# Raw rows transposed at the two feed-forward norms of a two-block model, with the inverse roots applied behind the products

## The reference

```python
# block 1 (D_FF = 2816)
h = h + concatenate([y_a, y_b, y_c]) @ w_out
hn = rms_norm(h, ffn_norm)               # h * rsqrt(mean(h*h) + eps) * gain
h = h + (silu(hn @ w_gate) * (hn @ w_up)) @ w_down
h = rms_norm(h, final_norm)
# block 2 (D_FF_2 = 4096)
x = x + mix @ w_out_2
h2 = rmsnorm(x, norm_mlp)
x = x + square(relu(h2 @ w_up_2)) @ w_down_2
```

## Time and profile before

| | us |
|---|---|
| median of three runs | 999.0 (997.72 to 999.48) |
| the profiled execution, its own time | 1003.03 |
| its span, first to last instruction | 1001.2 |
| TensorE busy | 931.7 (93%) |
| VectorE busy | 610.0 (61%) |
| ScalarE busy | 465.6 (47%) |
| GpSimd busy | 153.6 (15%) |

### The profile page before, as it was taken

One profiled execution on the slowest core, in us unless ns is written; L12 is line 12 of the kernel. 1 busy time (PEld: TensorE's weight loads), 2 busy tenths in 40 slices (PEclk: granted clock), 3 DMA queues, 4 the chain that ended last, 5 costly groups with the idle time before them and its releaser, 6 DMA issues. The chain is left out here.

```text
span 1001.2 us, 17392 instructions
## 1 busy us (share of the span) xinstructions
PE 931.7 (93%) x6836; PEld 826.8 (83%) x6836; DVE 610.0 (61%) x1288; ACT 465.6 (47%) x906; POOL 153.6 (15%) x111
## 2 busy tenths in 40 slices
PE   4999897999999969989699999898999979999998
PEld 2997686999999959879688888897888779999996
DVE  4557656556445577459877977626756656544553
ACT  5454545535444455363334674353453445444441
POOL 2000000000000014001775314000000004222321
PEclk9999998999999989999799999999999989999999
DMA  8540332564566434363432201202546436555451
GB/s 307 166 138 1 114 118 85 169 209 164 175 193 209 156 105 139 135 252 113 162 127 86 64 13 43 86 3 85 176 160 193 146 124 207 193 190 168 169 189 42
DMA packets 38677, 139.60 MB, mean 139 GB/s; under 512 B 4330, under 2 KB 4586, under 8 KB 38596
## 3 DMA queue, kind: packets, MB, share of 16 engines
q1 hardware_dynamic: 37184, 134.17, 39.8%
q10 hardware_dynamic: 884, 2.49, 0.7%
q0 software_dynamic: 528, 1.84, 0.6%
HBM read 137.39 MB, written 1.08 MB: 138 GB/s over the span
## 5 line engine op out<-in xcount | busy, mean ns | idle before, releaser
L1642 DVE TENSOR_TENSOR parts<-raw,parts 128x1024 fp32r<-128x1024 f32 (+1 forms) x227 | 291.1, 1319 | 170.5 <-ACT parts L1166 169.2
L1166 ACT ACTIVATE parts<-raw 128x1024 fp32r<-128x1024 f32 (+1 forms) x227 | 229.8, 1048 | 114.9 <-PE psum L504 104.9
L502 PE MATMUL psum<-hT,parts 128*128 128x256 f32 (+1 forms) x928 | 265.5, 286 | 10.2 <-DVE scr L2052 9.4
L503 PE MATMUL psum<-hT,parts 128*128 128x256 f32 (+1 forms) x928 | 264.1, 285 | 0.0
L504 PE MATMUL psum<-hT,parts 128*128 128x256 f32 (+1 forms) x928 | 262.3, 283 | 0.0
L502 PEld LDWEIGHTS psum<-hT,parts 128*128 128x128 f32 x928 | 176.6, 190 | 13.3 <-DVE scr L2052 9.6
L504 PEld LDWEIGHTS psum<-hT,parts 128*128 128x128 f32 x928 | 177.6, 191 | 0.0
L503 PEld LDWEIGHTS psum<-hT,parts 128*128 128x128 f32 x928 | 176.9, 191 | 0.5
L502 PE MATMUL psum<-parts,arena_r 128*128 128x512 f32 x344 | 137.1, 399 | 3.6 <-issue 3.0
L504 PE MATMUL psum<-parts,arena_r 128*128 128x512 f32 x344 | 136.5, 397 | 0.0
L503 PE MATMUL psum<-parts,arena_r 128*128 128x512 f32 x344 | 136.4, 396 | 0.0
(11 more groups left out here) (293 smaller groups left out, 1158.4 us busy)
## 6 DMA issues: line engine op xcount, KB each, us to landing
raw<-weights SPq DMA_DIRECT2D x247, 512.0 KB, 4.2
raw<-weights SPq DMA_DIRECT2D x4, 384.0 KB, 7.9
X<-x SPq DMA_DIRECT2D x2, 512.0 KB, 6.4
out<-X SPq DMA_DIRECT2D x2, 512.0 KB, 2.6
arena<-lines POOLq DMA_DIRECT2D x1, 768.0 KB, 10.3
cbuf<-consts ACTq DMA_DIRECT2D x1, 561.0 KB, 5.3
arena<-lines POOLq DMA_DIRECT2D x1, 544.0 KB, 7.6
arena<-params ACTq DMA_DIRECT2D x1, 512.0 KB, 9.0
```

Of the source, the lines that this page charges most:

```text
L502: mm(ps, a, c, start=start, stop=False)
L503: mm(ps, a, d, start=False, stop=False)
L1166: signal(A(split_slot(name)[0], whole_piece, ACT.Copy), "first_parts")
L1642: signal(V_.tensor_tensor(second, whole_piece, first.bitcast(F32), ALU.subtract), "split_vector")
```

## The change

The transposes at both feed-forward norms read X itself, before any scaling, and in two column halves. `first_rows(0)` (k = 0 to 3) is issued inside the second half of the projection, behind piece j = 2; `first_rows(1)` (k = 4 to 7) is issued inside the first product (`gate.0`), ahead of its k = 4. `last_rows` does the same in block 2, inside `out2_1` and `up2.0`. The residual adds and the copies out of PSUM follow in the same halves. The half sums and the inverse root come behind all copies.

In block 1 TensorE spreads the two columns of inverse roots over all partitions (`inverse_rows`: a column broadcast to 128 x 128 against the identity), behind `up1.0`. ScalarE copies this row tile of 256 columns twice side by side, and VectorE multiplies the whole bank `gu_f` (512 columns) by it into SBUF, ahead of silu. In block 2 the square of relu carries the factor twice, and the last residual multiplies by its square, one number per token.

```diff
-        ffn1 = lay(0, [("Xn", TT * D), ("sg", 4 * SEQ), ("v", 4 * SEQ)])
+        ffn1 = lay(0, [("Xn", TT * D), ("gu", 4 * 2 * SEQ), ("rows", 2 * SEQ)])
...
-            def feature_product(name, cols, ps, acts=hT):
+            def feature_product(name, cols, ps, acts=hT, ahead_of={}):
                 w = [half.rearrange("p (k n) -> p k n", k=KD) for half in split(name)]
                 for k in range(KD):
+                    if k in ahead_of:
+                        ahead_of[k]()
                     need(k)
...
+            def rows_turned(tag, job, nh):
+                for t in range(TT):
+                    freed(pe, job(nh, t))
+                transposes_of(X, lambda k: f"{tag}_{k}", ks=range(4 * nh, 4 * nh + 4))
+
+            def first_rows(nh):
+                rows_turned("norm2", lambda nh, t: f"o12_{nh}_{t}", nh)
+
+            out1_part(2, 0)
+            out1_part(2, 1, lambda: first_rows(0))
...
-            norm_turn("norm2", 1, ffn1["Xn"].rearrange("p (t n) -> p t n", t=TT))
...
+            def inverse_rows():
+                pe.wait_ge(sem("rms2"), 1)
+                ps = opened("rows2")
+                for t in range(TT):
+                    last = mm(ps[:, P * t:P * t + P], st[:, 4 + t:5 + t].to_broadcast([P, P]), ident, start=True, stop=True)
+                closed(last, "rows2")
...
-                done_with(f"gate.{f}", feature_product(f"gate.{f}", tok, ps[:, 0:SEQ]))
+                done_with(f"gate.{f}", feature_product(f"gate.{f}", tok, ps[:, 0:SEQ],
+                                                       ahead_of={4: lambda: first_rows(1)} if f == 0 else {}))
+                if f == 0:
+                    turn[0], turn[1] = 0, 4
                 closed(feature_product(f"up1.{f}", tok, ps[:, SEQ:2 * SEQ]), name)
                 piece_used[f"up1.{f}"] = name
+                if f == 0:
+                    inverse_rows()
...
+            def last_rows(nh):
+                rows_turned("norm4", lambda nh, t: f"o2_{nh}_{t}", nh)
+
+            two_tokens("out2_0", "o2_0", mixT)
+            two_tokens("out2_1", "o2_1", mixT, lambda: last_rows(0))
+            late_rows = {4: lambda: last_rows(1)}
...
# ScalarE, block 1
+            turned_out(lambda k: f"norm2_{k}", hT, SEQ, lambda k: par("ffn_norm")[:, k:k + 1])
             half_sums("sq2", lambda t, nh: f"o12_{nh}_{t}", ffn1["Xn"].rearrange("p (t n) -> p t n", t=TT))
-            second_tile("2", ffn1["Xn"].rearrange("p (t n) -> p t n", t=TT))
-            turned_out(lambda k: f"norm2_{k}", hT, SEQ, lambda k: par("ffn_norm")[:, k:k + 1])
...
+            full(act, "rows2")
+            rows = ffn1["rows"].rearrange("p (s n) -> p s n", s=2)
+            step_ = A(rows[:, 0, :], bank_of("rows2")[:, 0:SEQ], ACT.Copy)
+            signal(step_, "rows_out")
+            release(A(rows[:, 1, :], bank_of("rows2")[:, 0:SEQ], ACT.Copy), "rows2")
+            gu = ffn1["gu"].rearrange("p (s w n) -> p s w n", s=4, w=2)
             for f in range(FT1):
                 full(act, f"gu_{f}")
-                if f >= 4:
-                    freed(act, f"gu_{f - 4}")
-                signal(A(sg[:, f % 4, :], bank_of(f"gu_{f}")[:, 0:SEQ], ACT.Silu), "silu1")
                 freed(act, f"gu_{f}")
-                signal(A(aT[:, 0, f, :], v1[:, f % 4, :], ACT.Copy), "hidden1_first")
+                signal(A(gu[:, f % 4, 0, :], gu[:, f % 4, 0, :], ACT.Silu), "silu1")
+                act.wait_ge(sem("gated1"), f + 1)
+                signal(A(aT[:, 0, f, :], gu[:, f % 4, 1, :], ACT.Copy), "hidden1_first")
...
# VectorE, block 1
-            residual([(t, nh, f"o12_{nh}_{t}") for nh in range(2) for t in range(TT)])
-            norm_rows("norm2", ffn1["Xn"].rearrange("p (t n) -> p t n", t=TT), "sq2")
-            turned_rest(lambda k: f"norm2_{k}", hT, SEQ, lambda k: par("ffn_norm")[:, k:k + 1])
+            for nh in range(2):
+                residual([(t, nh, f"o12_{nh}_{t}") for t in range(TT)], nh == 0)
+                turned_rest(lambda k: f"norm2_{k}", hT, SEQ, lambda k: par("ffn_norm")[:, k:k + 1], range(4 * nh, 4 * nh + 4))
+            dve.wait_ge(sem("sq2"), 2 * TT)
+            link(V_.tensor_tensor(st[:, 0:2], st[:, 0:2], st[:, 2:4], ALU.add))
+            inv_rms(st[:, 4:6], st[:, 0:2], D, st[:, 6:8], st[:, 8:10], "rms2")
...
             def hidden_rest(f):
+                dve.wait_ge(sem("silu1"), f + 1)
+                u = gu[:, f % 4, 1, :]
+                signal(V_.tensor_tensor(u, u, gu[:, f % 4, 0, :], ALU.mult), "gated1")
                 dve.wait_ge(sem("hidden1_first"), f + 1)
-                signal(V_.tensor_tensor(aT[:, 1, f, :], v1[:, f % 4, :], aT[:, 0, f, :].bitcast(F32), ALU.subtract), "hidden1")
+                signal(V_.tensor_tensor(aT[:, 1, f, :], u, aT[:, 0, f, :].bitcast(F32), ALU.subtract), "hidden1")
+            freed(dve, "rows2")
             for f in range(FT1):
                 full(dve, f"gu_{f}")
-                dve.wait_ge(sem("silu1"), f + 1)
-                release(V_.tensor_tensor(v1[:, f % 4, :], bank_of(f"gu_{f}")[:, SEQ:2 * SEQ], sg[:, f % 4, :], ALU.mult),
-                        f"gu_{f}")
+                release(V_.tensor_tensor(ffn1["gu"].rearrange("p (s n) -> p s n", s=4)[:, f % 4, :], bank_of(f"gu_{f}"),
+                                         ffn1["rows"], ALU.mult), f"gu_{f}")
                 hidden_rest(f)
...
# VectorE, block 2: halves as above with o2_, norm4 and norm_mlp, then
+            inv_rms(st[:, 4:6], st[:, 0:2], D, st[:, 6:8], st[:, 8:10])
+            link(V_.tensor_tensor(st[:, 10:12], st[:, 4:6], st[:, 4:6], ALU.mult))
...
-            residual([(t, nh, f"d2_{t}_{nh}") for t in range(TT) for nh in range(2)])
+                    release(V_.scalar_tensor_tensor(out=xs, in0=bank_of(name), scalar=st[:, 10 + t:11 + t], in1=xs,
+                                                    op0=ALU.mult, op1=ALU.add), name)
```

More of the change, by code:

```diff
@@ L511, in need, with transposes_of @@
                     freed(pe, arrivals.pop(k))
-            def transposes_of(src, name_of, gain_tiles=KD, meta=None, turn_of=lambda k: ident):
-                for k in range(gain_tiles):
+            def transposes_of(src, name_of, meta=None, turn_of=lambda k: ident, ks=range(KD)):
+                for k in ks:
                     name = name_of(k)
@@ L534, in feature_product, with token_products @@
                 return last
-            def token_products(unit, tiles, acts, width=512):
+            def token_products(unit, tiles, acts, width=512, amid=None):
                 for job, cols in tiles:
@@ L553, in token_products @@
                         done_with(name, last)
+                    if j == 2 and amid:
+                        amid()
             def scores(g):
@@ L720, in y_turns, with out1_part @@
                     arrivals[k] = name
-            def out1_part(part, nh):
+            def out1_part(part, nh, amid=None):
                 js = OUT_PARTS[part]
@@ L741, in out1_part @@
                         done_with(name, last)
+                        if amid:
+                            amid()
             def swa_heads():
@@ L781, in _ @@
             y_turns(range(YM, KD))
-            for nh in range(2):
-                out1_part(2, nh)
+            def rows_turned(tag, job, nh):
[6 more added lines that the diff above has]
+            out1_part(2, 1, lambda: first_rows(0))
             def norm_turn(tag, count, src):
@@ L824, in down @@
                     done_with(f"{what}.{f}", last)
-            turn[0], turn[1] = 0, 4
+            def inverse_rows():
[4 more added lines that the diff above has]
+                closed(last, "rows2")
             def hidden1(f0, nf):
@@ L845, in _, with two_tokens @@
             norm_turn("norm3", 1, two["Xn"].rearrange("p (t n) -> p t n", t=TT))
-            def two_tokens(uname, tag, acts=hT):
-                token_products(uname, [(f"{tag}_{t}", tiles2[t]) for t in range(TT)], acts)
+            def two_tokens(uname, tag, acts=hT, amid=None):
+                token_products(uname, [(f"{tag}_{t}", tiles2[t]) for t in range(TT)], acts, amid=amid)
             def small_products():
@@ L1103, in _ @@
             transposes_of(mix, lambda k: f"mixT_{k}")
-            for n in range(2):
-                two_tokens(f"out2_{n}", f"o2_{n}", mixT)
-            norm_turn("norm4", 1, dn["Vb"].rearrange("p (t n) -> p t n", t=TT))
-            turn[0], turn[1] = 0, 4
+            def last_rows(nh):
[3 more added lines that the diff above has]
+            late_rows = {4: lambda: last_rows(1)}
             for n in range(8):
@@ L1112, in _ @@
                     ps = opened(name)
-                    done_with(f"up2.{2 * j}", feature_product(f"up2.{2 * j}", tok, ps[:, 0:SEQ]))
+                    done_with(f"up2.{2 * j}", feature_product(f"up2.{2 * j}", tok, ps[:, 0:SEQ],
+                                                              ahead_of=late_rows if j == 0 else {}))
+                    if j == 0:
+                        turn[0], turn[1] = 0, 4
```

(21 more changed lines are left out.)

5 lines of the change are left out of this document (1 added, 4 removed).

## The result

The changed kernel took 994.3 us (median of 10 runs, 989.8 to 996.2) beside 999.0 us before on the same chip (10 runs): ratio 0.9942, 95% interval 0.9923 to 0.9961. So it is faster, by 4.7 us; the forecast was 988.0 us and 11.0 us. In two further measurements beside the kernel before it took 991.3 and 995.6 us, ratios 0.9921 (0.9902 to 0.9940) and 0.9947 (0.9926 to 0.9967). Its 22 timed runs in these three measurements lie in two groups: ten at 989.8 to 992.5 us with a mean granted clock of 0.986 to 0.990, and twelve at 994.1 to 996.6 us with 0.979 to 0.983.

A forecast was written before the change was run, and what follows sets the result against it. TensorE, busy 93% of the span, was taken to bound the kernel, so only its gaps could be won. Terms -5.0 (first norm), -6.1 (second norm) and +0.1 (end) gave -11.0 from 999.0: 988.0 us, range 985.0 to 993.0.

The forecast's parts named there:

- First norm: Block 1's feed-forward norm: `gate.1` starts at 174.65 instead of 179.71, 5.0 us won.
- adds at 165.85: First norm: VectorE's two residual adds of columns 512 to 1023 start at 165.85, behind a weight split, and take 1.39 us.
- stall ahead of the roots: First norm, behind `up1.0`: TensorE waits 1.0 us for VectorE's inverse-root chain before the matmuls that spread the roots.
- the lower bound for the half sums: First norm, ScalarE: four half sums at 0.63 us each, ending at 171.8; 0 to 0.8 us more was possible.
- spreading matmuls: First norm: two matmuls spreading the inverse roots over the rows, taken as 0.25 us from two warm transposes.
- Second norm to `up2.1`: Block 2's feed-forward norm: the first product ends at 813.1 instead of 819.21, 6.1 us won.
- gate and up covered: Gate and up loop: VectorE needs at most 5.1 us of TensorE's 5.7 us per tile; the opposing rival had chance 0.04.
- the end: Last four residual adds, now with a per-partition factor: 0 to 0.07 us extra each, 0.1 us taken in all.
- clock rival at the norms: New short TensorE waits at the norms drop the clock, losing 2.2 us a norm: 990 to 992.5 us; chance 0.14.
- No spread of roots follows here: Second norm: sums and chain run beside products until about 817; only the last four adds want their factor.
- each microsecond saved at a norm moves the end by the same amount: Whole kernel: TensorE hardly waits elsewhere, so norm savings pass fully to the end if other engines keep up.
- the last line of the sum: Whole kernel: the summed change of -11.0 us taken from the timed 999.0 us, giving 988.0 us; chance 0.60.

The follow-up runs named there:

- bank kernel: Changed kernel with PSUM banks turned from 1, not 0, after the second norm's first up product: 988.92 us, then 992.73 us in a repeat.
- roots_later: Changed kernel with the two matmuls that spread the inverse roots one tile later, between `gate.1` and `up1.1`: 989.35 us.
- wide: Changed kernel with the 64-column matmuls behind norm 3 made 128 columns wide: 991.76 us, then 992.59 us in a repeat.
- first half: Changed kernel with its second norm and last adds put back as before the change: 995.85 us, ratio 0.9968.
- all four: Changed kernel with banks turned from 1, inverse roots one tile later, unread matmuls ahead of norm 3 and 128-column products behind it: 986.75 us.
- narrow later: Changed kernel with 8 unread 256-column matmuls ahead of the 64- and 128-column products behind norm 3, which so come 0.9 us later: 995.51 us.
- second half: Changed kernel with its first norm and gate and up loop put back as before the change: 995.24 us, ratio 0.9957.
- filler: Changed kernel with 60 unread 256-column matmuls in TensorE's wait ahead of norm 3's transposes: 990.31 us, ratio 0.9907.

## Why the prediction was wrong

**The local steps were right.** First norm: 5.0 us forecast, 5.1 measured. The single steps: adds at 165.85 forecast and 166.63 less 0.83 = 165.8 measured; 1.0 us of stall ahead of the roots forecast, 0.8 measured (174.96 less 174.04 less a pitch of 0.12; 0.64 of it put down to VectorE). The last half sum ended at 172.38 less 0.83 = 171.55, where 171.8 was reckoned, so the lower bound for the half sums was the right one. The spreading matmuls took 0.47 us (174.96 to 175.43), where 0.25 was reckoned from two transposes. These small errors cancel, by luck. Second norm to `up2.1`: 6.1 us forecast and measured. The 512-column product took 0.69 us, as taken from the add of the same shape; gate and up covered; the end 0.06 us a pair, 0.1 in all.

**The clock rival at the norms was wrong.** The short waits left the clock at the upper level in all profiles of the new form (twelve of each norm). The rule of the Trainium skill, "TensorE: Matmul & The Clock Gate", section "A second HAM failure mode: psum-queue depth-cycling", that frequent short idles make it swing, did not hold for these.

**One wait was missed.** "No spread of roots follows here" was true, but the bank counter is set back behind the first up product, and the first tile's bank is bank 0 already. Before, the reset stood ahead of it, and the two tiles had banks 0 and 1. The wait cost 0.84 us, and without it the bank kernel won 1.0.

**The step that failed** is the sentence "each microsecond saved at a norm moves the end by the same amount", and the last line of the sum, which took -11.0 from the median. The fixed part of the change is 207.24 - 202.19 = 5.05 us and 196.9 - 191.8 = 5.1 us, 10.15 in all. The time of the rest of the program isn't fixed:

```
profile            ahead of norm 1  low clock   middle  low clock   wait  middle less wait
roots_later             160.7          3.4       411.8    20.5      6.1       405.7
wide                    160.8          3.4       411.4    17.1      6.7       404.7
changed, third          161.5          6.8       416.9    27.3      8.3       408.6
before                  161.7          6.8       413.9    20.5      9.4       404.5
changed, second         161.8          6.8       415.6    30.7      6.3       409.2
bank                    161.8          6.8       412.0    20.5      5.9       406.1
changed, first          162.5          6.8       416.0    27.3      7.5       408.6
first half              162.7          6.8       414.1    27.3      5.6       408.5
bank, again             162.9         10.2       413.7    20.5      9.2       404.5
all four                162.9         10.2       412.7    17.1      8.3       404.4
narrow later            163.3         10.2       417.8    27.3      9.2       408.5
second half             163.9         13.7       411.0    17.1      6.8       404.2
wide, again             164.1         13.7       412.4    20.5      7.3       405.0
filler                  164.1         13.7       410.0    13.7      5.7       404.3
```

(us; low clock is the sum of stretches at 0.50 in the trace's clock record; the middle is from norm 3's transposes to those of the mixed heads, its low clock counted from 8 us ahead; the wait is TensorE's longest in the middle, some 110 us behind its start.) The code ahead of norm 1 is the same in all fourteen, and takes 160.7 to 164.1 us in the order of its low-clock time.

In the middle two things vary, and neither is a part of the change. One is the wait. TensorE stands at about 475 us until VectorE has made two pairs of weight splits (L1672) and what follows them; TensorE's product behind the wait and the second pair of splits in the bank kernel's two profiles, first and second:

```profile
472.58 3.81 DVE L1672 TENSOR_TENSOR parts<-raw,parts 128x1024 fp32r<-128x1024 f32 x2 [1.64 <-ACT parts L1196]
480.01 0.58 PE L502 MATMUL psum<-hT,parts 128*128 128x256 f32 x1 [5.90 <-DVE scr L2088]
```

```profile
475.30 5.06 DVE L1672 TENSOR_TENSOR parts<-raw,parts 128x1024 fp32r<-128x1024 f32 x2 [1.64 <-ACT parts L1196]
476.09 3.19 POOL L1613 TENSOR_TENSOR parts<-raw,parts 128x1024 fp32r<-128x1024 f32 x1
483.99 0.58 PE L502 MATMUL psum<-hT,parts 128*128 128x256 f32 x1 [9.20 <-DVE scr L2088]
```

A split takes VectorE 1.22 us; those beside which GpSimd makes a split of its own (L1613) take longer by about the time of the overlap, up to 3.41 us. In all fourteen profiles the sum of the four splits ahead of the wait, 6.9 to 10.9 us, is the wait plus 1.3 to 1.5 us. So this is where 5.6 to 9.4 us of wait come from; what sets the two engines' splits beside each other in one execution and not in the next stays open. The other thing is the clock: less the wait, the middle took 408.5 to 409.2 us in the five profiles with 27 us or more at the lower level in it (the later form's 408.5 holds 0.9 us of added matmuls), and 404.2 to 406.1 us in the nine with 20.5 or less. In the changed kernel's three profiles it is so 4.1 to 4.7 us longer than in the one from before (408.6 to 409.2 for 404.5), and a wait shorter by 1.1 to 3.1 us hides part of it.

What that did to the times can be reckoned from the timed runs. By the means the changed kernel gained 5.6, 7.8 and 5.2 us in the three measurements, 6.1 us over its 22 runs. In the second and third, where each run's clock is on record for both kernels, the means are 999.70 us at clock 0.9818 (30 runs before) and 993.16 us at 0.9852 (12 of the changed kernel), a gain of 6.5 us. The low stretches at the two norms, 6.8 us each in every profile with the old form, are gone; alone they would raise the mean clock by 13.7 x 0.5 / 1000 = 0.0068. It rose by 0.0034. So about 0.0034 x 994 / 0.5 = 6.8 us more were spent at the lower level elsewhere, worth up to 3.4 us where TensorE is busy; 10.15 - 6.5 = 3.6 us are missing. That the clock took them in the timed runs is worked out, not shown by an edit, and how long the wait at 475 us was in them isn't known. Why the changed kernel has the lower clock more often than its neighbours (12 of 22 runs at 0.983 or less, 2 of 10 of the bank kernel, none of 4 with the roots later) stays open: chance of the executions and the position of its narrow products are both left.

The first measurement, 4.7 us, shows less than the mean of all, since six of its ten runs have clock 0.983 or less. Even the mean gain, 6.1 us, is 4.9 us short of the forecast: 0.84 us by the missed wait; the other 4 us lie in code that the change doesn't touch, most of it put down to the clock by the sum above.

## What to carry to other kernels

A gain at one place of a program that TensorE bounds is safe only as a local number: read it between two fixed marks of the trace, where it mostly repeats to hundredths, and expect the whole to move by it plus or minus what low-clock stretches and waits elsewhere do (the 22 runs of the changed kernel spread over 6.8 us). When two profiles of the same code differ, take out the longest wait first and see what is left for the clock. Look at the clock of each timed run before an edit is credited, and repeat the baseline in another measurement. Where jobs are moved across a reset of a buffer counter, write down which buffer each one gets on both sides of it.

## What was not expected of the hardware

The granted clock fell to 0.50 while TensorE was busy in every microsecond, behind the 32 matmuls of 64 and 128 columns (in four of fourteen profiles, each time within 0.1 us of the start of the last one), and stayed there for 3.4 us, which is 1.7 us of work. It did not fall for waits of 0.24, 0.60 and 0.64 us within 7.5 us at the first norm. Matmuls that nobody reads, put into a wait of 7.6 us, kept it up. And a weight split of 1.22 us on VectorE took up to 3.41 us while GpSimd made one too, GpSimd's own 3.2 instead of 2.4.
